# Two layers on one core: the latents' norms in two halves, the index scores ahead of the RWKV rows, and feed-forwards that begin by channel block

## The reference

```
cq = rms_norm(c_q, q_norm); ckv = rms_norm(c_kv, kv_norm)
iq = einsum('btr,rhd->bthd', cq, w_idx_q); ik = rms_norm(idx_k_raw, idx_k_norm)
score = einsum('bth,bths->bts', wi, relu(einsum('bthd,bsd->bths', qi, ik)))
score = where(causal, score, -inf); _, sel = top_k(score, topk)      # topk = 256
...
p = p + mu_shift * (p_prev - p)          # RWKV columns, mixed with the token before
S = S * w_t + sa * b_t + v_t * k_t       # the scan over 1024 tokens
...
x = x + g_m * rms_norm(mix @ w_out, mix_post_norm)
hf = rms_norm(x, ffn_pre_norm) * (1 + sc_f) + sh_f
f = (silu(hf @ w_ffn_gate) * (hf @ w_ffn_up)) @ w_ffn_down
```

```
h = h + rms_norm(mixed @ w_o, g_mix_post); u2 = rms_norm(h, g_ffn_pre)
up = causal_dwconv3(u2 @ w_ffn_up, conv_ffn_w) + b_ffn_conv
h = h + rms_norm((gelu(f_gate) * f_val) @ w_ffn_down, g_ffn_post)
```

## Time and profile before

| | |
|---|---|
| median of 3 runs | 3649.11 us (3641.34 to 3659.92) |
| the profiled execution | 3646.83 us |
| its span in the trace | 3645.5 us |
| mean granted clock of PE in it | 0.962 |
| PE busy | 3346.4 us (92%) |
| DVE busy | 1794.3 us (49%) |
| ACT busy | 928.1 us (25%) |
| POOL busy | 339.0 us (9%) |
| PE in slices 5 to 8 of 40 (364 to 729 us) | 8, 6, 7, 8 tenths |
| DVE in slices 5 to 8 | 6, 7, 7, 6 tenths |
| POOL in slices 5 to 8 | 2, 4, 5, 7 tenths |

### The profile page before, as it was taken

One profiled execution on the slowest core, in us unless ns is written; L12 is line 12 of the kernel. 1 busy time (PEld: TensorE's weight loads), 2 busy tenths in 40 slices (PEclk: granted clock), 3 DMA queues, 4 the chain that ended last, 5 costly groups with the idle time before them and its releaser, 6 DMA issues.

```text
span 3645.5 us, 51038 instructions
## 1 busy us (share of the span) xinstructions
PE 3346.4 (92%) x21635; PEld 2602.0 (71%) x21650; DVE 1794.3 (49%) x2850; ACT 928.1 (25%) x1709; POOL 339.0 (9%) x278
## 2 busy tenths in 40 slices
PE   7988867887888999999999889999998999999998
PEld 6736655775567788888886556876676888878876
DVE  2378677664556322224545546321246444444656
ACT  2255432333534100001222544000025111111122
POOL 0000245762001000000000000000000000000000
PEclk9989977999999999999999999999999999999999
DMA  6337210101114111113331001111133111123434
GB/s 216 70 65 239 84 42 19 37 20 59 47 64 133 52 47 52 47 47 104 121 118 50 4 24 40 42 35 35 58 116 110 47 47 52 47 75 98 140 115 144
DMA packets 217381, 270.18 MB, mean 74 GB/s; under 512 B 11229, under 2 KB 176387, under 8 KB 216900
## 3 DMA queue, kind: packets, MB, share of 16 engines
q1 hardware_dynamic: 211851, 247.87, 21.3%
q10 hardware_dynamic: 3192, 11.17, 1.7%
q0 software_dynamic: 2112, 7.87, 0.6%
HBM read 232.80 MB, written 34.08 MB: 73 GB/s over the span
## 4 chain that ended last, share of the span: by engine, by line
PE 81%; DVE 11%; ACT 4%; issue 2%; DMA 1%; POOL 1%; SPq 0%; DVEq 0%; ACTq 0%; POOLq 0%
PE psum L2071 18%; PE psum L2073 18%; PE psum L2075 18%; PE psum L523 5%; PE psum L3089 3%; PE psum L1266 2%; PE psum L2589 2%; PE psum L2910 2%; PE psum L2797 2%; PE psum L651 1%; PE psum L1821 1%; PE psum L2926 1%; DVE Lg L1915 1%; PE psum L1847 1%; DMA slot<-in_ada_w 1%
## 5 line engine op out<-in xcount | busy, mean ns | idle before, releaser
L2071 PE MATMUL psum<-hT_hi,wcut_lo 128*128 128x512 f32 x1856 | 589.4, 395 | 16.7 <-DVE hT_lo L2110 16.7
L2073 PE MATMUL psum<-hT_hi,wcut_hi 128*128 128x512 f32 x1856 | 582.8, 391 | 0.0
L2075 PE MATMUL psum<-hT_lo,wcut_hi 128*128 128x512 f32 x1856 | 582.5, 391 | 0.0
L2071 PEld LDWEIGHTS psum<-hT_hi,wcut_lo 128*128 128x128 f32 x1856 | 350.4, 189 | 97.0 <-DVE hT_lo L2110 17.9
L2053 DVE CAST wcut_hi<-raw 128x1024 fp32r<-128x1024 f32 x256 | 176.9, 691 | 478.6 <-PE psum L2075 454.0
L2075 PEld LDWEIGHTS psum<-hT_lo,wcut_hi 128*128 128x128 f32 x1856 | 350.3, 189 | 73.2
L2073 PEld LDWEIGHTS psum<-hT_hi,wcut_hi 128*128 128x128 f32 x1856 | 350.3, 189 | 72.6
L2071 PE MATMUL psum<-wcut_hi,xcut_lo 128*128 128x512 f32 x1120 | 348.7, 393 | 17.6 <-DVE xcut_lo L2189 13.8
L2073 PE MATMUL psum<-wcut_hi,xcut_hi 128*128 128x512 f32 x1120 | 347.2, 392 | 0.0
L2075 PE MATMUL psum<-wcut_lo,xcut_hi 128*128 128x512 f32 x1120 | 346.9, 391 | 0.0
L1097 POOL TENSOR_TENSOR st<-st,nhalf 128x1 f32<-128x1 f32 (+2 forms) x78 | 61.1, 790 | 2827.2 <-DVE st L709 2827.2
(11 more groups left out here) (428 smaller groups left out, 4354.5 us busy)
## 6 DMA issues: line engine op xcount, KB each, us to landing
raw<-in_w_ffn_down SPq DMA_DIRECT2D x88, 512.0 KB, 3.6
raw<-in_w_ffn_up SPq DMA_DIRECT2D x66, 512.0 KB, 3.8
slot<-in_ada_w SPq DMA_DIRECT2D x24, 1024.0 KB, 11.7
raw<-in_w_in SPq DMA_DIRECT2D x28, 512.0 KB, 5.4
raw<-in_w_ffn_gate SPq DMA_DIRECT2D x22, 512.0 KB, 3.9
slot<-in_w_in SPq DMA_DIRECT2D x8, 1024.0 KB, 6.1
raw<-in_w_out SPq DMA_DIRECT2D x16, 512.0 KB, 3.7
x_one<-xrow SPq DMA_DIRECT2D x16, 512.0 KB, 2.8
```

The lines of the kernel that those rows point to most:

```text
L2071: pe.matmul(outs[i], al, bs[i][0], start=start, stop=False, skip_group_check=True)
L2073: pe.matmul(outs[i], ah, bs[i][0], start=False, stop=False, skip_group_check=True)
L2075: mm = pe.matmul(outs[i], ah, bs[i][1], start=False, stop=stop, skip_group_check=True)
```

## The change

It has seven parts.

1. **Latents' norms.** `norms_vector` does them for tiles 0 to 3 between the evacuations of att 0 of tiles 4 to 6, and for tiles 4 to 7 behind; each half has its own squares (`sqs3`), one power on POOL for all three norms.
2. **Order in the projection.** `LAT_STEPS` now holds chunk 0's rows: five, then one after each two turns; then `iq`, then the scores, with nothing of `ROW_STEPS` between. The bias stands behind lora on PE and ACT. All 56 rows of `ROW_STEPS` follow. Modulation rows stand behind two of every three RWKV rows of chunks 1 to 3.
3. **Passes.** 180 lie beside rows (4 behind an RWKV row without a front round, 2 otherwise), 210 with lora's; `best_steps` is 2 and 13 are left for the rounds 7 to 13.
4. **Loads.** Other slots; the latents' store comes behind `("rkv", 2)`, the RWKV weights' 11 transfers behind the eleventh modulation weight of the list (before: behind `("rkv", 4)`). The wait for the bias table goes to `rwkv_rows` and `front_vector`.
5. **POOL.** `keys_pool(t + 1)` stands behind the values of tile `t` (for tile 1 behind front round 5 of tile 0, in the projection); tile 0's values come in round 7, ahead of `free_pool`.
6. **ACT.** Front rounds 5 and later of tile 0 are ahead of the counts of the same step.
7. **Feed-forward start.** For a half, each channel block `k` is transposed for four tiles into one bank (`turn_block`), emptied by one 128x512 instruction (`scaled_vector`), split by `high_scalar` and `low_vector`, and used for all three weights at once. The other half's norms stand between by `k`. A weight's `used` comes at its last `k`, so all three come at the end.

The diff, cut to its core:

```diff
-LAT_STEPS = [("turn", t) for t in range(NT)] + [("iq", q) for q in range(4)]
+
+LAT_STEPS = [("rkv", 0, t) for t in range(5)] + [("turn", 0), ("turn", 1), ("rkv", 0, 5), ("turn", 2), ("turn", 3), ("rkv", 0, 6),
+             ("turn", 4), ("turn", 5), ("rkv", 0, 7), ("turn", 6), ("turn", 7)] + [("iq", q) for q in range(4)]
+LAT_BANK, _n = [], [0, 0]
+for _s in LAT_STEPS:
+    _row = _s[0] == "rkv"
+    LAT_BANK.append((6, 7, 0, 1)[_n[1] % 4] if _row else 2 + 2 * (_n[0] % 2))
+    _n[_row] += 1
...
-        if (1, 5) <= (_c, _t) < (3, 5):
+        if _c < 4 and (8 * _c - 8 + _t) % 3:
...
-SLOT_OF = {_s: (1, 3, 4)[_i % 3] for _i, _s in enumerate(_mods)}
-SLOT_OF.update({("rkv", _c): 2 * (_c % 2) for _c in range(2, 6)})
+SLOT_OF = {_s: 1 + _i % 3 for _i, _s in enumerate(_mods)}
+SLOT_OF.update({("rkv", _c): 4 * (_c % 2) for _c in range(1, 6)})
...
-ROW_BANK = [6 + i % 2 if i < ROWS_FIRST else 2 + i % 6 if i < BESIDE else 2 + i % 5 for i in range(len(ROW_STEPS))]
+ROW_BANK = [2 + i % 6 if i < BESIDE else 2 + i % 5 for i in range(len(ROW_STEPS))]
...
+        if key == ("rkv", 2):
+            latents_store(sp, K)
+        if key == MODS[10]:
             rwkv_weights(sp, K)
...
+    for step, b in zip(LAT_STEPS, LAT_BANK):
+        lat_tensor(pe, K, step, b)
...
+    pe.wait_ge(*D["hot"].at("hot"))
+    for i, o in enumerate(range(0, 1152, 512)):
+        n = min(512, 1152 - o)
+        pe.wait_ge(*B.free(2 * i))
+        mm = pe.matmul(bank(K, 2 * i)[0:8, 0:n], K.relb[0:33, :], K.oh[0:33, o:o + n], start=True, stop=True, skip_group_check=True)
+        B.until(2 * i, S, ("bias", i))
+    mm.then_inc(*T.up("bias"))
+    for i in range(len(ROW_STEPS) + 1):
...
+        if 4 <= t < 7:
+            norms_vector(v, K, 0, t - 4)
+    for part in range(3):
+        norms_vector(v, K, 1, part)
+    V.mark("latents")
...
+def norms_vector(v, K, hf, part):
+
+    V = K.V
+    ts_ = slice(4 * hf, 4 * hf + 4)
+    if part == 0:
+        v.wait_ge(*K.S.at(("att", 1, 4 * hf + 3)))
+        v.wait_ge(*V.own())
+        for j, (a, n) in enumerate(LATENTS):
+            x_, sq = K.att[:, ts_, a:a + n], K.sqs3[j]
+            v.tensor_tensor(sq, x_, x_, MUL).then_inc(*V.up())
+            v.wait_ge(*V.own())
+            v.tensor_reduce(K.st[:, 4 * j:4 * j + 4], sq, AX, ADD).then_inc(*V.up())
+        v.wait_ge(*V.own())
+        for j, (a, n) in enumerate(LATENTS):
+            variance(v, K, ("lv", hf), K.st[:, 4 * j:4 * j + 4], n, 1e-6)
+    if part == 1:
+        v.wait_ge(*K.G.at(("lr", hf)))
+        for j, dst in enumerate((K.att[:, ts_, 0:256], K.ckv[:, ts_, :], K.ikk[:, ts_, 0:64])):
+            a, n = LATENTS[j]
+            v.tensor_tensor(dst, K.att[:, ts_, a:a + n], K.st[:, 16 + 4 * j:20 + 4 * j].unsqueeze(2).to_broadcast([128, 4, n]), MUL).then_inc(
+                *V.up(("latents divided", hf)))
+    if part == 2:
+        v.wait_ge(*V.own())
+        v.wait_ge(*K.D["m2"].at("m2"))
+        v.tensor_tensor(K.ckv[:, ts_, :], K.ckv[:, ts_, :], K.kvB.unsqueeze(1).to_broadcast([128, 4, 128]), MUL).then_inc(*V.up())
+        ikk = K.ikk[:, ts_, 0:64]
+        v.tensor_tensor(ikk, ikk, K.ikB.unsqueeze(1).to_broadcast([128, 4, 64]), MUL).then_inc(*V.up())
+        v.wait_ge(*V.own())
+        v.tensor_copy(K.ikk[:, ts_, 64:128], ikk).then_inc(*V.up())
+        v.tensor_scalar(K.iw[:, ts_, :], K.att[:, ts_, 448:456], float(8 ** -0.5 * 64 ** -0.5), None, MUL).then_inc(*V.up())
...
-    return 4 if ROW_STEPS[i - 1][0] == "rkv" and i <= BESIDE else 2
+    return 4 if i and ROW_STEPS[i - 1][0] == "rkv" and round_beside(i) is None else 2
...
+        if j is not None and j >= 5:
+            front_scalar(s, K, 0, j)
...
+            if round_beside(i) == 5:
+                keys_pool(g, K, 1)
...
-    return 3 if g < 14 else 2
+    return 2
...
-VALUES, VALUES_FIRST = 6, 8
+VALUES, VALUES_FIRST = 6, 7
+
+
+def keys_pool(g, K, t):
+
+    G = K.G
+    g.wait_ge(*K.D["raw"].at(t))
+    g.tensor_tensor(K.prev, K.prev, K.mx, SUB).then_inc(*G.up())
+    g.wait_ge(*G.own())
+    g.tensor_tensor(K.prev, K.prev, K.muB, MUL).then_inc(*G.up(("mixed", t)))
...
+    if t and j == VALUES and t + 1 < NT:
+        keys_pool(g, K, t + 1)
...
+def turn_block(pe, K, P, h, k, b):
+    for t in range(4 * h, 4 * h + 4):
+        if k == 0:
+            pe.wait_ge(*K.S.at(("normed", P.name, t)))
+        if t == 4 * h:
+            pe.wait_ge(*K.bank.free(b))
+        tr = pe.transpose(bank(K, b)[:, t % 4 * 128:t % 4 * 128 + 128], P.y[:, t, k * 128:(k + 1) * 128], K.ident)
+    tr.then_inc(*K.T.up(("turned block", P.name, h, k)))
+    K.turn_bank[P.name, h, k] = b
+    K.bank.until(b, K.V, ("scaled block", P.name, h, k))
+
+
 def ffn_start_tensor(pe, K, name, P):
-
-    for t in range(4):
-        post_turn(pe, K, P, t, (2 * t, 2 * t + 1))
-    channel_block(pe, K, name, 0, 0, (0,))
-    channel_block(pe, K, name, 1, 2, (0,))
-    post_turn(pe, K, P, 4, (6, 7))
-    channel_block(pe, K, name, 2, 4, (0,))
-    post_turn(pe, K, P, 5, (1, 3))
-    post_turn(pe, K, P, 6, (6, 7))
-    post_turn(pe, K, P, 7, (1, 3))
     for n in range(3):
-        channel_block(pe, K, name, n, 2 * n, (1,))
+        pe.wait_ge(*K.V.at(("cut", name, n)))
+    for h in range(2):
+        ahead = len(TURN_BANKS[h])
+        for k in range(ahead):
+            turn_block(pe, K, P, h, k, TURN_BANKS[h][k])
+        for n in range(3):
+            pe.wait_ge(*K.bank.free(2 * n + h))
+        for k in range(8):
+            pe.wait_ge(*K.V.at(("split", name, h, k)))
+            for n in range(3):
+                wh, wl = weight_pair(K, name, n)
+                mm = product3(pe, [bank(K, 2 * n + h)], (wh[:, k, :], wl[:, k, :]), [(K.hi[:, k, tokens(h)], K.lo[:, k, tokens(h)])],
+                              k == 0, k == 7)
+                if h and k == 7:
+                    mm.then_inc(*K.T.up(("used", name, n)))
+            if k + ahead < 8:
+                turn_block(pe, K, P, h, k + ahead, TURN_BANKS[h][k % ahead])
+
+
+def scaled_vector(v, K, P, h, k):
+    v.wait_ge(*K.T.at(("turned block", P.name, h, k)))
+    v.tensor_scalar(P.turned[:, k, tokens(h)], bank(K, K.turn_bank[P.name, h, k]), K.AB[:, P.a, k:k + 1],
+                    K.AB[:, P.b, k:k + 1] if P.b is not None else 0.0, MUL, ADD).then_inc(*K.V.up(("scaled block", P.name, h, k)))
+
+
+def low_vector(v, K, P, h, k):
+
+    if k == 0:
+        scaled_vector(v, K, P, h, 0)
+    if k < 7:
+        scaled_vector(v, K, P, h, k + 1)
+    v.wait_ge(*K.V.at(("scaled block", P.name, h, k)))
+    v.wait_ge(*K.S.at(("split", P.after, h, k)))
+    v.tensor_tensor(K.lo[:, k, tokens(h)], P.turned[:, k, tokens(h)], K.hi[:, k, tokens(h)].bitcast(F), SUB).then_inc(
+        *K.V.up(("split", P.after, h, k)))
...
 def ffn_start_vector(v, K, name, P):
     cut_to(v, K, name, 2)
-    for t in range(4):
-        post_out_vector(v, K, P, t)
-    v.wait_ge(*K.S.at(("turned out", name, 0)))
-    split_vector(v, K, name, P.turned, (0,))
-    tail_vector(v, K, P)
-    v.wait_ge(*K.S.at(("turned out", name, 1)))
-    split_vector(v, K, name, P.turned, (1,))
+    for k in range(8):
+        low_vector(v, K, P, 0, k)
+        if 1 <= k:
+            if k in (1, 2, 4, 6):
+                if k >= 4:
+                    post_mean2(v, K, P, k // 2 + 2)
+                post_mean(v, K, P, 4 + (1, 2, 4, 6).index(k))
+            if k in (2, 3, 5, 7):
+                post_sum(v, K, P, 4 + (2, 3, 5, 7).index(k))
+    for t in (6, 7):
+        post_mean2(v, K, P, t)
+    for k in range(8):
+        low_vector(v, K, P, 1, k)
 
 
 def ffn_start_scalar(s, K, name, P):
-    for t in range(4):
-        post_out_scalar(s, K, P, t)
-    split_scalar(s, K, name, P.turned, (0,))
-    tail_scalar(s, K, P)
-    split_scalar(s, K, name, P.turned, (1,))
+    for k in range(8):
+        high_scalar(s, K, P, 0, k)
+        if k in (1, 2, 4, 5):
+            post_square(s, K, P, 4 + (1, 2, 4, 5).index(k))
+        if k in (3, 4, 6):
+            post_square2(s, K, P, 4 + (3, 4, 6).index(k))
+        if k in (5, 7):
+            post_norm(s, K, P, 4 + (5, 7).index(k))
+    post_square2(s, K, P, 7)
+    for t in (6, 7):
+        post_norm(s, K, P, t)
+    for k in range(8):
+        high_scalar(s, K, P, 1, k)
```

More of the change, by code:

```diff
@@ L799, in proj_vector @@
         for _ in range(passes_beside(i)):
-            next(K.best)
-        if ROW_STEPS[i - 1][0] == "mod":
+            next(K.best, None)
+        if i and ROW_STEPS[i - 1][0] == "mod":
             mod_vector(v, K, ROW_STEPS[i - 1], ROW_BANK[i - 1])
@@ L1039, in proj_scalar @@
             next(K.sums, None)
-    for i in range(ROWS_FIRST, len(ROW_STEPS) + 1):
+    s.wait_ge(*T.at("bias"))
+    for i, o in enumerate(range(0, 1152, 512)):
+        n = min(512, 1152 - o)
+        s.activation(K.oh[0:8, o:o + n], bank(K, 2 * i)[0:8, 0:n], ACT.Copy).then_inc(*S.up(("bias", i)))
+    s.wait_ge(*S.own())
+    s.dma_start(K.vbd.ap(), K.oh[0:8, :].unsqueeze(1).to_broadcast([8, 128, 1152])).then_inc(*D["bias"].up("bias", 16))
```

(8 more changed lines are left out.)

124 lines of the change are left out of this document (42 added, 82 removed).

## The result

The changed kernel took 3688.62 us (median of 4, 3682.88 to 3699.12) against 3645.23 for the kernel before on the same chip: 1.0109 times, interval 1.008 to 1.0138. It is 43 us slower, where 61 to 64 faster was forecast. Its profiled execution has a span of 3682.2 us at a mean clock of 0.963; before it was 3645.5 at 0.962.

The account below looks back on a forecast made before the run. PE, busy 92% of the span, was taken as the bound, so gains lay where it waits or runs slowly. A 14, B 42, C 7 and D 1 sum to 64 off 3646.8, 3582.8, given as 3584 us, range 3552 to 3620.

Parts of the forecast that it names:

- A: Projection (99 to 443 us): removed waits of 20.1 less new costs of 6.3, a gain of 14, range 3 to 24.
- the bias's third bank: Projection: a new wait, as ACT frees this bank only after a lora half, some 1.3 us.
- all five: Rivals: projection pays back nothing; rounds shrink more; rounds hang on a chain; slower through ACT's queue; feed-forwards don't start earlier.
- rival 4: Projection: ACT's queue couples search counts and rows, 2.3 us a round wiping out 64; 3660 to 3690 us, chance 0.04.
- The signs of being wrong: Projection waits for ACT's evacuations over 15 us, a second interval over 45, or first feed-forward matmul at its old distance.
- The near tie of PE and DVE: Projection: DVE's work ends at 417, nearly level with PE's end, so A's gain could fall to 3.
- rival 1: Projection pays back nothing, A's waits returning for the other engine: 3597 us, up to 3627; chance 0.18.
- Rival 2: RWKV rounds shrink more as the clock rises: 54 from B, 20 from A, 3546 to 3563 us; chance 0.13.
- C: First feed-forward's start: block-wise transposes and earlier norms, a gain of 7, range 0 to 9.
- D: Second feed-forward's start: C's 7 less 5.9 for the unhidden cut 3, a gain of 1, range -6 to 3.
- B: RWKV rounds: with 13 passes, not 53, four tiles take 178.4, not 220.71; gain 42, range 33.7 to 54.
- the wait of 10.9 for vrow: RWKV rounds: PE's wait for POOL's vrow, expected to go because vrow is made ahead of free_pool, one round sooner.

Follow-up runs that it names:

- bias_early: Changed kernel with the bias products, evacuation and 4.6 MB transfer back behind the first five rows of chunk 0: 3622.47 us, 0.9927 of the kernel before.
- bias_head: Changed kernel, bias still late, but only the first head's rows written there, the other seven heads' at about 105 us: 3620.45 us (one execution).
- weights_late: Changed kernel with SP's eleven loads of rwkv_weights four modulation weights later, the bias write left in place: 3689.96 us (one execution).
- passes_back: Kernel with early bias and low part ahead, but 3 search passes beside RWKV rows (not 4) and 3 in rounds 7 to 13: 3608.22 us.
- mended_more: Kernel with early bias and low part ahead, plus PE's cut-weight wait behind the first transposes and an earlier weight 3 cut in feed-forward two: 3584.03 us.

## Why the prediction was wrong

**A, the step that failed.** The text lists for the moved bias "the bias's third bank" and prices it at 1.3. It counts three products and three evacuations and leaves out the fourth thing that the step issues: the transfer of 4.6 MB to `bias_rows`, which lay in a stretch in which PE waited for no load, and so cost nothing. At the new place it runs beside the ring's loads, which feed PE within a few microseconds. That is the wait of 70.2, more than the whole gain of 64; bias_early and bias_head show it. The kernel has the line, and the view of transfers shows its size and the 62.3 us of the one load beside it. No rival had it either: all five are about engines, and of the queues only SP's issues were priced, at 2. The time lies in rival 4's 3660 to 3690, but by luck: its mechanism, counts and rows holding each other up on ACT, did not cost 64, for with the bias early, and search and rows as changed, the first mark came sooner than before the change. The signs of being wrong would not have found it either: they name waits for ACT, the second interval and the first product, and no wait for a load. A second error in the same paragraph: MODS[10] is the third of the sixteen modulation weights that are left, not the eleventh, as the list counts the first eight too; so the eleven loads stand ahead of thirteen slots, not of five. By weights_late this is worth at most some 3 us at the first mark.

**A, the rest.** With the bias early the first mark is 12.1 sooner than before the change; 14 was forecast. Scores at 146.14 (145), lora's end at 233.88 (238). The late bias's own waits were 5.36 and 4.16, where 1.3 was taken: PE waits for ACT's lora, which stands behind counts, and then for its own evacuation. The near tie of PE and DVE did not turn into rival 1. Rival 2's time does not follow from its terms: 54, 20 and the 8 of C and D are 82, which gives 3565, not 3546 to 3563.

**The keys on POOL.** The price was put at 1 to 2 us by a row in which three passes lost 0.5 together, and the rule of the Trainium skill (page "SBUF — State Buffer", section "SBUF: two separate sides"), by which the working came to up to 4.7, was set aside. The runs agree with the rule: the two mask passes, which read two tiles of SBUF, took 2.52 and 2.59 and not 0.56, 4.0 us more together, and ended only behind POOL's instructions. The first mark moved by 6.1; where the other 2.1 come from was not traced. The row that I used is of passes with one tile as input, and the instruction of POOL beside them was one of 1.28 us, not of 2.34. The same timeline, just before that row, had the better one (DVE and POOL, kernel before): a small instruction with two inputs, 0.17 us elsewhere, took 1.22 and ended with POOL's.

```profile
414.71 1.25 POOL L1682 TENSOR_TENSOR tmp<-mx,krow 128x512 f32<-128x512 f32 x1
416.04 1.28 POOL L1684 TENSOR_TENSOR tmp<-tmp,rowB 128x512 f32<-128x512 f32 x1
```

```profile
414.77 1.22 DVE L915 SCALAR_TENSOR_TENSOR top<-top 128x6 f32<-128x6 f32 x1
```

**B was right**: 178.4 forecast, 178.2 measured, and each of the four within 1.6 (54, 38, 42, 44.35; 53.56, 37.54, 41.18, 45.89). passes_back shows that most of it is the passes. One part of its working was wrong: the wait of 10.9 for vrow was counted as won, and POOL's new order is worth 6.1 in the first interval, 1.8 net at the second mark and nothing at the eighth. The 54 for the first interval was a round figure and did not suffer by it, which is luck in part.

**C and D.** The first product came 4.1 us sooner after w_out (4.4 forecast), and the second half's first product 12.4 sooner (11.4 forecast). Then the working says "All of half 1 is then done at 1205", 20.8 us for 72 products. It took 33.7, from 1202.86 to 1236.5, and 23.0 with the low part ahead, and that is the failed step of C and D: the half was costed by a window in which nothing had to be made for PE, and the chain of transposes, emptying and low part was not followed through the order of DVE's list with two banks. With the order mended, C is a gain of 6.6 (7 forecast) and D a loss of 1.7 (a gain of 1 forecast); the wait for the cut of weight 3 behind the convolution was seen rightly (4.4).

Put together, the change with the transfer and the order mended gives 3596, 12 above the forecast of 3584, and the measured 3688.62 is what one transfer (75.6 at the first mark) and one order (10.6 and 8.1) make of it. That mended_more comes to 3584.03 is luck: it takes out a wait that the forecast had counted as staying.

## What to carry over

When a step is moved, list what it issues last, its transfers too, and look up for each how long it runs and what ran beside it: a transfer that cost nothing did so at its own place. Then ask how long the loads beside it took to land, and who waits for those at the new place. Where a stage is cut into blocks that several engines pass on, follow one block through each engine's list in order, with the number of banks, before taking a full-speed window as its price.
